# Down products of three FFN phases by seven block products instead of eight, with the upper halves' low parts by accumulating DMA

## The chip, the cores and the metric

The kernel runs as one program on one core of a Trainium2 chip. The metric is its device time in microseconds. The kernel before took 1877.66 us, the median of three runs (1875.56 to 1878.22).

## The reference, cut to what matters

Two layers over 528 tokens (16 learned meta tokens and 512 of the sequence) of width 1024; each layer has two SwiGLU half steps (FFNs) with a mixer between them, and a layer norm after each of the three. The change touches only the FFNs, four in all. D_FF is 2816, that is 22 hidden tiles of 128.

```python
def swiglu(x, w_gate, w_up, w_down):
    return (jax.nn.silu(x @ w_gate) * (x @ w_up)) @ w_down

for l in range(DEPTH):
    h = layer_norm(a * h + 0.5 * swiglu(h, ffn1_w_gate[l], ffn1_w_up[l], ffn1_w_down[l]), ln1_g[l], ln1_b[l])
    ...   # projection, causal pooling, gated linear attention, w_out
    h = layer_norm(a * h + y, ln2_g[l], ln2_b[l])
    h = layer_norm(a * h + 0.5 * swiglu(h, ffn2_w_gate[l], ffn2_w_up[l], ffn2_w_down[l]), ln3_g[l], ln3_b[l])
return h[:, N_META:]
```

## The kernel before

Everything is stored transposed: 8 blocks of 128 channels on the partitions, tokens along the free axis. Each float32 operand is split into a high part (the value copied to fp32r) and a low part (value minus high part), and each product is three matmuls: high x high, high x low, low x high. The last FFN computes only the 512 own tokens (span OWN), the other three all 528 (span ALL, in two halves of 264).

Weights come as one stream of pieces of 128 x 1024 floats (512 KB). SP loads them into two raw buffers (`raw`, L337), each as soon as the piece that was in it is split; ScalarE makes the high part in one of four slots of `w_hi` (`high_part`, L927) once the piece four before is used up; the low part comes from VectorE (L1280, pieces of the fast pairs), from GpSimd by a subtraction (L358, the classic gate and up pieces and all down pieces), or, for mixer pieces and the first four of an FFN, by ScalarE writing the negated weights into `w_lo` (L933) and GpSimd issuing a DMA that adds the weights from memory (L351).

An FFN goes through its 22 hidden tiles in three phases (8, 8, 6). For each tile m of a phase it computes gate and up, silu(gate) x up is the hidden tile (`prod`, then `h_hi`, `h_lo`), and at the end of the phase the down products of its tiles are added into X, eight output rows mo with all three matmuls for each tile (L411 to L413). Tiles 0 to 3 are classic: 96 matmuls a pair of gate and up. From tile 4 on a pair is a fast pair (`fast_pair`): the 2 x 2 block product of (gate, up) weights, each cut into a lower and an upper half of four channel blocks, with (early, late) halves of the tokens is made with seven products of 12 matmuls instead of eight. That wants four sums of weight blocks per pair (`w_sums`, VectorE; high parts by ScalarE L921, low parts by VectorE L1285), four sums of token blocks once per FFN (`v_sum`), and sums of the products in PSUM: ScalarE copies p1, u2 and p5 (L968, L980, L983), VectorE adds to c22 (L1337) and c12 (L1344). TensorE waits for p1_copied before its third product, u2_copied before the fifth, p5_copied before the sixth and c22_done before the seventh.

Each engine's order is written out by hand in its `ffn`: during pair i ScalarE and VectorE prepare the weights of pair i + 1 and finish the hidden tile of pair i - 1. `F22` and the counts in the waits number the tiles, `piece_done` the pieces that TensorE has used up. After the last phase the down rows end in `resid`, which also adds up the statistics for the layer norm.

Of the kernel before, what the change touches and what calls it, by code (L numbers as in the profile page):

```python
# [6 lines left out]

# [21 lines left out]
PHASES = ((0, 8), (8, 8), (16, 6))  # L29
# [27 lines left out]
FFN_PIECES = 2 * MT + len(PHASES) * KC  # L57
# [16 lines left out]
CLASSIC = 4  # L74
BAND = 4
BLOCK = BAND * P
FAST = MT - CLASSIC
# [24 lines left out]
def fast_index(l, f, m):  # L102

    return (2 * l + f) * FAST + m - CLASSIC


def whole(n):

    r = n % LAYER_PIECES
    if FFN_PIECES <= r < FFN_PIECES + MIX_IN + MIX_OUT:  # L110
        return True
    r -= 0 if r < FFN_PIECES else FFN_PIECES + MIX_IN + MIX_OUT
    for p, (m0, nm) in enumerate(PHASES):
        at = 2 * m0 + KC * p
        if at <= r < at + 2 * nm:
            return m0 + (r - at) // 2 < CLASSIC
    return True


def by_dma(n):  # L120

    r = n % LAYER_PIECES
    return n >= SLOTS and (r < SLOTS or FFN_PIECES <= r < FFN_PIECES + MIX_IN + MIX_OUT + SLOTS)


def lo_value(n):

    same = [i for i in range(n % SLOTS, n + 1, SLOTS) if by_dma(i) == by_dma(n)]
    return len(same) * (16 if by_dma(n) else 1)


def negated(n):

    return sum(by_dma(i) for i in range(n + 1))
# [38 lines left out]
def build(nc, x_t, stream, params, out_t):  # L173
    ctx = ExitStack()
    with ctx:
# [12 lines left out]
        x_lo = sb("x_lo", [P, KC, T], F32R)  # L188
# [33 lines left out]
        with ExitStack() as s4:  # L222
            v_sum = sb("v_sum", [P, 4, BAND, HALF], F32, s4)
        with ExitStack() as s5:
            s_hi = sb("s_hi", [P, 4, BLOCK], F32R, s5)
            s_lo = sb("s_lo", [P, 4, BLOCK], F32R, s5)
# [7 lines left out]
        with ExitStack() as s3:  # L234
            h_hi = sb("h_hi", [P, TILES, T], F32R, s3)
            h_lo = sb("h_lo", [P, TILES, T], F32R, s3)
            silu = sb("silu", [P, T], F32, s3)
# [3 lines left out]
            p5_copy = sb("p5_copy", [P, 2, HALF], F32, s3)  # L241
            u2_copy = sb("u2_copy", [P, 2, HALF], F32, s3)
# [37 lines left out]

        def matmul_parts(ps, span):
# [18 lines left out]
            s_sum_done s_hi_done s_lo_done v_sum_done v_hi_done v_lo_done""".split()  # L300
# [9 lines left out]

        def wait_piece(eng, n):

            eng.wait_ge((lo_added if by_dma(n) else lo_done)[n % SLOTS], lo_value(n))
# [10 lines left out]
        def _(sp):  # L324
# [7 lines left out]
            for n in range(SLOTS + RAWS, DEPTH * LAYER_PIECES):  # L332
                if by_dma(n - RAWS):
                    sp.wait_ge(S["raw_neg"], negated(n - RAWS))
                else:
                    wait_piece(sp, n - RAWS)
                sp.dma_start(raw[:, n % RAWS, :], stream[n // RAWS, n % RAWS]).then_inc(raw_full[n % RAWS], 16)  # L337
# [8 lines left out]
        def _(pool):  # L346
            def add_raw(n):

                slot = n % SLOTS
                pool.wait_ge(S["raw_neg"], negated(n))  # L350
                pool.dma_start(w_lo[:, slot, :], stream[n // RAWS, n % RAWS],  # L351
# [39 lines left out]
            for n in range(SLOTS, DEPTH * LAYER_PIECES):  # L391
                if n % LAYER_PIECES == FFN_PIECES + SLOTS:
                    pad(n // LAYER_PIECES)
                if by_dma(n):
                    add_raw(n)
                elif whole(n):
# [9 lines left out]
        def _(pe):  # L406
# [61 lines left out]
            def fast_product(o, hi, lo, rhs_hi, rhs_lo, start, stop):  # L468

                for k in range(BAND):  # L470
                    w = slice(k * P, (k + 1) * P)
                    nc.tensor.matmul(o, hi[:, w], rhs_hi[:, k, :], start=start and k == 0, stop=False,  # L472
                                     skip_group_check=True)
                    nc.tensor.matmul(o, hi[:, w], rhs_lo[:, k, :], start=False, stop=False, skip_group_check=True)  # L474
                    m = nc.tensor.matmul(o, lo[:, w], rhs_hi[:, k, :], start=False, stop=stop and k == BAND - 1,  # L475
                                         skip_group_check=True)
                return m

            def fast_pair(l, f, m, gate, span):
# [7 lines left out]
                low, high = slice(0, BLOCK), slice(BLOCK, 2 * BLOCK)  # L487
                g, u = gate % SLOTS, (gate + 1) % SLOTS
                x_low = (x_hi[:, 0:BAND, early], x_lo[:, 0:BAND, early])
                x_high = (x_hi[:, BAND:KC, early], x_lo[:, BAND:KC, early])  # L490
                x_late = (x_hi[:, BAND:KC, late], x_lo[:, BAND:KC, late])

                def mixed(j):
                    return v_hi[:, j - 1, :, 0:n], v_lo[:, j - 1, :, 0:n]

                def summed(j):
                    pe.wait_ge(S["s_lo_done"], 4 * i + j)
                    return s_hi[:, j - 1, :], s_lo[:, j - 1, :]

                wait_piece(pe, gate)  # L500
                fast_product(u0, w_hi[:, g, low], w_lo[:, g, low], *x_low, True, True).then_inc(S["p1_acc"], 1)
                pe.wait_ge(S["v_lo_done"], 4 * (2 * l + f) + 4)
                fast_product(g1, *summed(1), *mixed(1), True, True).then_inc(S["p5_acc"], 1)
                pe.wait_ge(S["p1_copied"], i + 1)
# [1361 lines left out]
```

## Time and profile before

| | |
|---|---|
| median of 3 runs | 1877.66 us (1875.56 to 1878.22) |
| profiled execution | 1878.16 us, its span 1876.4 us |
| mean granted TensorE clock | 0.991 of full speed |
| TensorE, matmuls | 1838.4 us busy, 14406 |
| VectorE | 1179.2 us busy, 1837 instructions |
| ScalarE | 881.3 us busy, 1357 |
| GpSimd | 351.7 us busy, 206 |
| DMA | 206.73 MB, 110 GB/s over the span |
| raw loads | 316 of 512 KB, 3.8 us from issue to landing (median) |
| accumulating loads | 60 of 512 KB, 7.8 us |

The page is one execution as the hardware profiler recorded it. Matmuls overlap in their pipeline, so the distance between two starts says what one costs, not its recorded duration; the same holds to a lesser degree for VectorE and ScalarE, whose instructions start before the one ahead has ended. In the rows, PE is TensorE, DVE VectorE, ACT ScalarE, POOL GpSimd, SPq the DMA queue of SP; `x2` in a timeline row are two instructions of that line back to back.

### The profile page before, as it was taken

The numbers are of one execution on the slowest core, as the hardware profiler recorded it, in microseconds if no ns is written. First come the engines' busy times: TensorE is split into PE (matmuls) and PEld (weight loads), VectorE is DVE, ScalarE is ACT, GpSimd is POOL, SyncE is SP. The second block draws the span as 40 slices with busy tenths as digits, with TensorE's granted clock in tenths as the row PEclk, the third lists the DMA queues.
The fourth block names the chain that finished last, engine by engine and source line by source line (L and its number), as shares of the span: only waits on it lengthen the run. The fifth ranks groups of instructions, "written<-read, shape, count | busy, mean of one in ns | idle before, by whom it ended". The sixth has DMA issues, their size and how long they took to land.

```text
span 1876.4 us, 34684 instructions
## 1 busy us (share of the span) xinstructions
PE 1838.4 (98%) x14406; PEld 1768.9 (94%) x14406; DVE 1179.2 (63%) x1837; ACT 881.3 (47%) x1357; POOL 351.7 (19%) x206
## 2 busy tenths in 40 slices
PE   8999999999999999999999999999999999999997
PEld 7999999999999999999999999999998879899895
DVE  5828638568547827728477286375684587285575
ACT  4524525474346524525465245254743465254353
POOL 3040220411002040130420302104110120303113
PEclk9999999999999999999999999999999999999998
DMA  4223323556554332332542333226565633333232
GB/s 158 102 90 113 102 81 111 154 121 132 112 126 97 103 103 91 106 93 96 144 103 102 91 113 107 89 99 158 128 134 113 133 89 102 99 109 119 82 111 90
DMA packets 57469, 206.73 MB, mean 110 GB/s; under 512 B 6368, under 2 KB 6368, under 8 KB 57312
## 3 DMA queue, kind: packets, MB, share of 16 engines
q1 hardware_dynamic: 48240, 171.78, 29.6%
q0 software_dynamic: 8640, 31.46, 9.2%
q8 instruction: 115, 1.88, 0.4%
q10 hardware_dynamic: 432, 1.25, 0.2%
q14 instruction: 42, 0.34, 0.1%
HBM read 202.38 MB, written 2.10 MB: 109 GB/s over the span
## 4 chain that ended last, share of the span: by engine, by line
PE 90%; DVE 5%; ACT 2%; DMA 1%; issue 1%; ACTq 0%; DVEq 0%
PE PS L472 12%; PE PS L475 12%; PE PS L474 12%; PE PS L411 9%; PE PS L412 9%; PE PS L413 9%; PE PS L452 5%; PE PS L453 5%; PE PS L454 5%; PE PS L443 2%; PE PS L421 2%; PE PS L422 2%; PE PS L737 1%; DMA raw<-in_stream 1%; ACT X L1064 1%
## 5 line engine op out<-in xcount | busy, mean ns | idle before, releaser
L358 POOL TENSOR_TENSOR w_lo<-raw,w_hi 128x1024 fp32r<-128x1024 f32 x112 | 282.1, 2523 | 1086.1 <-ACT w_hi L927 1059.8
L411 PE MATMUL PS<-h_hi,w_hi 128*128 128x264 f32 (+1 forms) x1238 | 370.2, 299 | 0.6 <-DVE h_lo L1219 0.3
L412 PE MATMUL PS<-h_lo,w_hi 128*128 128x264 f32 (+1 forms) x1238 | 369.7, 299 | 0.0
L413 PE MATMUL PS<-h_hi,w_lo 128*128 128x264 f32 (+1 forms) x1238 | 369.4, 298 | 0.0
L927 ACT ACTIVATE w_hi<-raw 128x1024 fp32r<-128x1024 f32 x240 | 215.1, 929 | 232.4 <-PE PS L413 179.2
L472 PE MATMUL PS<-v_hi,s_hi 128*128 128x264 f32 (+1 forms) x864 | 244.9, 283 | 0.2 <-ACT PS L968 0.2
L474 PE MATMUL PS<-v_lo,s_hi 128*128 128x264 f32 (+1 forms) x864 | 244.3, 283 | 0.0
L475 PE MATMUL PS<-v_hi,s_lo 128*128 128x264 f32 (+1 forms) x864 | 243.9, 282 | 0.0
L411 PEld LDWEIGHTS PS<-h_hi,w_hi 128*128 128x128 f32 x1238 | 233.0, 188 | 9.2 <-DVE h_lo L1219 1.7
L412 PEld LDWEIGHTS PS<-h_lo,w_hi 128*128 128x128 f32 x1238 | 233.1, 188 | 7.3
L413 PEld LDWEIGHTS PS<-h_hi,w_lo 128*128 128x128 f32 x1238 | 232.3, 188 | 7.3
L921 ACT ACTIVATE s_hi<-s_sum 128x512 fp32r<-128x512 f32 x288 | 177.9, 631 | 100.2 <-PE PS L475 96.1
L452 PE MATMUL PS<-x_hi,w_hi 128*128 128x264 f32 (+1 forms) x696 | 208.1, 299 | 1.7 <-ACT s_r L1154 1.6
L453 PE MATMUL PS<-x_lo,w_hi 128*128 128x264 f32 (+1 forms) x696 | 205.9, 296 | 0.0
L454 PE MATMUL PS<-x_hi,w_lo 128*128 128x264 f32 (+1 forms) x696 | 205.6, 295 | 0.0
L1285 DVE TENSOR_TENSOR s_lo<-s_sum,s_hi 128x512 fp32r<-128x512 f32 x288 | 190.3, 686 | 16.5 <-ACT s_hi L921 15.9
L475 PE MATMUL PS<-x_hi,w_lo 128*128 128x264 f32 (+1 forms) x576 | 163.1, 283 | 0.0
L472 PEld LDWEIGHTS PS<-v_hi,s_hi 128*128 128x128 f32 x864 | 162.5, 188 | 0.4 <-ACT PS L968 0.4
L474 PEld LDWEIGHTS PS<-v_lo,s_hi 128*128 128x128 f32 x864 | 162.9, 189 | 0.0
L472 PE MATMUL PS<-x_hi,w_hi 128*128 128x264 f32 (+1 forms) x576 | 162.7, 283 | 0.0
L475 PEld LDWEIGHTS PS<-v_hi,s_lo 128*128 128x128 f32 x864 | 162.4, 188 | 0.0
L474 PE MATMUL PS<-x_lo,w_hi 128*128 128x264 f32 (+1 forms) x576 | 161.5, 280 | 0.0
(231 smaller groups left out, 4107.8 us busy)
## 6 DMA issues: line engine op xcount, KB each, us to landing
raw<-in_stream SPq DMA_DIRECT2D x316, 512.0 KB, 3.8
w_lo<-in_stream POOLq DMA_DIRECT2D x60, 512.0 KB, 7.8
raw_first<-in_stream SPq DMA_DIRECT2D x4, 512.0 KB, 5.9
out_t<-X SPq DMA_DIRECT2D x8, 256.0 KB, 2.1
X<-in_x_t SPq DMA_DIRECT2D x7, 264.0 KB, 7.5
par<-in_params ACTq DMA_DIRECT2D x2, 480.0 KB, 3.5
X<-in_x_t ACTq DMA_DIRECT2D x1, 264.0 KB, 4.8
```

Source lines behind the costliest of these rows:

```text
L358: nc.gpsimd.tensor_tensor(w_lo[:, slot, :], raw[:, slot % RAWS, :], w_hi[:, slot, :].bitcast(F32), ALU.subtract).then_inc(lo_done[slot], 1)
L411: nc.tensor.matmul(o, hi, rhs_hi[:, k, tok], start=first, stop=False)
L412: nc.tensor.matmul(o, hi, rhs_lo[:, k, tok], start=False, stop=False)
L413: return nc.tensor.matmul(o, lo, rhs_hi[:, k, tok], start=False, stop=last)
L452: yield nc.tensor.matmul(o, hi, rhs_hi[:, k, tok], start=k == 0, stop=False)
L453: yield nc.tensor.matmul(o, hi, rhs_lo[:, k, tok], start=False, stop=False)
L454: yield nc.tensor.matmul(o, lo, rhs_hi[:, k, tok], start=False, stop=k == n - 1)
L472: nc.tensor.matmul(o, hi[:, w], rhs_hi[:, k, :], start=start and k == 0, stop=False, skip_group_check=True)
L474: nc.tensor.matmul(o, hi[:, w], rhs_lo[:, k, :], start=False, stop=False, skip_group_check=True)
L475: m = nc.tensor.matmul(o, lo[:, w], rhs_hi[:, k, :], start=False, stop=stop and k == BAND - 1, skip_group_check=True)
L927: nc.scalar.activation(w_hi[:, n % SLOTS, part], raw[:, n % RAWS, part], ACT.Copy).then_inc(S["raw_hi"], 1)
L1285: V.tensor_tensor(s_lo[:, j - 1, :], s_sum[:, j - 1, :], s_hi[:, j - 1, :].bitcast(F32), ALU.subtract).then_inc(S["s_lo_done"], 1)
```

## The change

The phases become (6, 6, 6, 4). The down products of the first three phases are also made as 2 x 2 block products: two output rows (mo = 2q and 2q + 1) against the early and late tokens, with the phase's six tiles cut into those with an even and those with an odd place (three each). A phase has four such down pairs of 7 x 9 = 63 matmuls. They take the place of a pair in `FAST_ORDER`, one pair later than the phase's last tile: the first gate and up pair of the next phase comes before them. So each engine runs one loop over 30 fast pairs of an FFN, 18 of gate and up and 12 down. Down pairs need the weight sums as the others do (three blocks of 128 wide), and four sums of each pair of hidden tiles (`t_sums`), with their high and low parts (`t_hi`, `t_lo`). Their results go into X by two VectorE instructions (`add_down`). The last phase's four tiles stay classic, two rows to a piece.

The low parts of the upper halves of a fast pair's weights come in the other way: ScalarE writes the negated half (`negative`), GpSimd issues an accumulating DMA of that half (256 KB, 192 KB for a down pair); VectorE makes only the gate's lower half. SP's reload waits for the negated half and for the weight sums too. `p5_copy` and `u2_copy` have one buffer instead of two; raw hidden tiles share storage with their low parts.

```diff
-PHASES = ((0, 8), (8, 8), (16, 6))
+PHASES = ((0, 6), (6, 6), (12, 6), (18, 4))
+def fast_order():
+    order = []
+    for p, (m0, nm) in enumerate(PHASES):
+        order += [("up", m, 0) for m in range(CLASSIC if p == 0 else m0 + 1, m0 + nm)]
+        if p < FAST_DOWNS:
+            order.append(("up", m0 + nm, 0))
+            order += [("down", p, q) for q in range(PAIRS)]
+    return order
 @@ SP
+                if dma_adds(was):
+                    sp.wait_ge(S["raw_neg"], negated(was))
+                if engine_splits(was):
+                    wait_low(sp, was)
+                if kind_of(was) in ("gate", "up"):
+                    sp.wait_ge(S["s_sum_done"], 4 * fast_index(*place_of(was)) + (4 if kind_of(was) == "gate" else 2))
+                part = slice(0, width(n))
 @@ GpSimd
-                pool.dma_start(w_lo[:, slot, :], stream[n // RAWS, n % RAWS],
+                pool.dma_start(w_lo[:, slot, part], stream[n // RAWS, n % RAWS, :, part],
                                accum_op=ALU.add).then_inc(lo_added[slot], 16)
 @@ TensorE, fast_pair
+                wait_low(pe, gate)
+                if kind == "down":
+                    pe.wait_ge(S["h_lo_done"], l * 44 + 22 * f + sum(PHASES[a]))
                 ...                                     # p1
+                    pe.wait_ge(S["t_lo_done"], thirds_index(l, f, sum(PHASES[a]) - 1) + 1)
                 ...                                     # p5, p6
+                wait_added(pe, gate)
                 ...                                     # g0 with the gate's upper half, p7, p3
-                wait_piece(pe, gate + 1)
+                wait_added(pe, gate + 1)
                 pe.wait_ge(S["c22_done"], i_all + 1)
 @@ ScalarE, in fast pair i
                     act.wait_ge(S["p1_acc"], i_all + 1)
                     ...                                 # copy p1
+                    if was == "up":
+                        act.wait_ge(S["c12_done"], i_all)
+                        silu_of(2 - ps, layout)
+                    if follows:
+                        gate_high(fast_piece(l, f, i + 1))          # high part, then negated upper half
                     ...                                 # copies u2, p5
+                    if follows:
+                        up_high(fast_piece(l, f, i + 1) + 1)        # upper half: high part, negated
+                        for j in range(1, 4):
+                            sum_high(l, f, i + 1, j)
+                    if was == "up" and kind == "up":
+                        hidden_high(l, f, was_a, span)
+                    elif was == "down" and kind == "up":
+                        act.wait_ge(S["piece_done"], fast_piece(l, f, i))
+                        hidden_high(l, f, sum(PHASES[was_a]), span)
+                    if follows:
+                        sum_high(l, f, i + 1, 4)
 @@ VectorE
+            def t_sums(l, f, m, span):                  # after the product of each tile with odd place
+                V.tensor_tensor(t[2], b22, b12, ALU.subtract).then_inc(S["t_sum_done"], 1)
+                V.tensor_tensor(t[0], b11, b12, ALU.subtract).then_inc(S["t_sum_done"], 1)
+                dve.wait_ge(S["t_sum_done"], 4 * at + 1)
+                V.scalar_tensor_tensor(out=t[1], in0=t[2], scalar=-1.0, in1=b11, op0=ALU.mult, op1=ALU.subtract)
+                dve.wait_ge(S["t_sum_done"], 4 * at + 3)
+                V.scalar_tensor_tensor(out=t[3], in0=t[1], scalar=-1.0, in1=b21, op0=ALU.mult, op1=ALU.subtract)
+            def add_down(l, f, i, span):
+                for odd, op in enumerate((ALU.add, ALU.subtract)):
+                    x, y = halves(X[:, 2 * q + odd, :], halved(span)), pair(ps + odd, halved(span))
+                    ...                                 # ALPHA * x op y in phase 0, x op y after it
 @@ VectorE, in fast pair i
+                    if was == "down":
+                        add_down(l, f, i - 1, span)
+                    if follows:
+                        w_sums(l, f, i + 1)
+                    if was == "up":
+                        fast_prod(l, f, was_a, 2 - ps, span)        # and t_sums at an odd place
+                    if follows:
+                        gate_low(fast_piece(l, f, i + 1))           # lower half only
+                        sum_low(l, f, i + 1, 1)
                     ...                                 # c22, sum_low 2 and 3, c12
+                    if was == "up" and kind == "up":
+                        hidden_low(l, f, was_a, span)
+                    elif was == "down" and kind == "up":
+                        hidden_low(l, f, sum(PHASES[was_a]), span)
+                    if follows:
+                        sum_low(l, f, i + 1, 4)
 @@ TensorE, end of an FFN
+                last_down(0, range(nm - 1))
+                last_down(1, range(nm - 1))             # two rows before the last tile is wanted
+                last_down(0, [nm - 1]).then_inc(S["last_acc"], 1)
+                last_down(1, [nm - 1]).then_inc(S["piece_done"], 1)
```

## Rows read from the trace of the kernel before

**Rows 1.** First part of the page: busy us (share of the span) x instructions.

```profile
PE 1838.4 (98%) x14406; PEld 1768.9 (94%) x14406; DVE 1179.2 (63%) x1837; ACT 881.3 (47%) x1357; POOL 351.7 (19%) x206
```

**Rows 2.** Fourth part of the page: the chain that ended last, by engine.

```profile
PE 90%; DVE 5%; ACT 2%; DMA 1%; issue 1%; ACTq 0%; DVEq 0%
```

**Rows 3.** Waits of TensorE, whole span: waiting <- releaser: total us, times, longest.

```profile
PE PS L421 <- DVE w_lo L1781: 8.9, 3, 7.9
...
PE PS L472 <- DVE PS L1337: 1.1, 1, 1.1
```

**Rows 4.** Window, first FFN: length, busy us of each engine, clock, DMA.

```profile
30.00:340.00 310.00, 309.92 (x2559) 309.70 (x2558) 195.53 (x283) 140.46 (x237) 59.97 (x24) 1.00 0.31 100
```

**Rows 5.** Timeline, ScalarE's copy of p1: start us, us, instruction, idle before.

```profile
70.86 0.38 ACT L968 ACTIVATE PS<-PS 128x264 f32<-128x264 f32 x1 [2.22 <-PE PS L475]
...
81.05 0.38 ACT L968 ACTIVATE PS<-PS 128x264 f32<-128x264 f32 x1 [2.22 <-PE PS L475]
...
1654.00 0.37 ACT L968 ACTIVATE PS<-PS 128x256 f32<-128x256 f32 x1 [2.11 <-PE PS L475]
...
1663.81 0.37 ACT L968 ACTIVATE PS<-PS 128x256 f32<-128x256 f32 x1 [2.11 <-PE PS L475]
```

**Rows 6.** Timeline of VectorE, down rows added into X, two FFNs.

```profile
105.77 0.70 DVE L1365 SCALAR_TENSOR_TENSOR X<-X,PS 128x528 f32<-128x528 f32 x1 [2.17 <-PE PS L413]
111.57 0.70 DVE L1365 SCALAR_TENSOR_TENSOR X<-X,PS 128x528 f32<-128x528 f32 x1 [5.10 <-PE PS L413]
...
1609.38 0.69 DVE L1365 SCALAR_TENSOR_TENSOR X<-X,PS 128x512 f32<-128x512 f32 x1 [4.87 <-PE PS L413]
1614.94 0.69 DVE L1365 SCALAR_TENSOR_TENSOR X<-X,PS 128x512 f32<-128x512 f32 x1 [4.87 <-PE PS L413]
```

**Rows 7.** Timeline of VectorE, one pair of gate and up, first FFN.

```profile
70.67 0.69 DVE L1266 TENSOR_TENSOR s_sum<-raw 128x512 f32<-128x512 f32 x1 [1.30 <-DMA raw<-in_stream]
...
73.28 0.70 DVE L1214 SCALAR_TENSOR_TENSOR prod<-PS,silu 128x528 f32<-128x528 f32 x1
73.89 1.82 DVE L1280 TENSOR_TENSOR w_lo<-raw,w_hi 128x1024 fp32r<-128x1024 f32 x2
75.63 0.69 DVE L1285 TENSOR_TENSOR s_lo<-s_sum,s_hi 128x512 fp32r<-128x512 f32 x1
76.23 0.70 DVE L1219 TENSOR_TENSOR h_lo<-prod,h_hi 128x528 fp32r<-128x528 f32 x1
76.85 0.43 DVE L1337 TENSOR_TENSOR PS<-PS,p_copy 128x264 f32<-128x264 f32 x1
77.19 1.28 DVE L1285 TENSOR_TENSOR s_lo<-s_sum,s_hi 128x512 fp32r<-128x512 f32 x2
...
80.10 0.69 DVE L1266 TENSOR_TENSOR s_sum<-raw 128x512 f32<-128x512 f32 x1 [0.55 <-DMA raw<-in_stream]
```

**Rows 8.** Timeline of ScalarE, same pair.

```profile
71.64 1.58 ACT L927 ACTIVATE w_hi<-raw 128x1024 fp32r<-128x1024 f32 x2
...
74.33 0.63 ACT L921 ACTIVATE s_hi<-s_sum 128x512 fp32r<-128x512 f32 x1
74.85 0.65 ACT L909 ACTIVATE h_hi<-prod 128x528 fp32r<-128x528 f32 x1
```

**Rows 9.** Landing: raw loads 60:340, raw loads 395:505, accumulating loads.

```profile
DMA to landing us min/median/max: 3.3/3.7/6.1
...
DMA to landing us min/median/max: 3.8/4.2/9.6
...
DMA to landing us min/median/max: 6.5/7.8/10.4
```

**Rows 10.** Timeline of VectorE, first fast pair of the first FFN.

```profile
66.49 0.44 DVE L1337 TENSOR_TENSOR PS<-PS,p_copy 128x264 f32<-128x264 f32 x1
```

**Rows 11.** Timeline of VectorE, end of the first phase.

```profile
101.44 2.16 DVE L1219 TENSOR_TENSOR h_lo<-prod,h_hi 128x528 fp32r<-128x528 f32 x1 [0.71 <-ACT h_hi L909]
```

**Rows 12.** Timeline of GpSimd, same stretch.

```profile
100.62 2.40 POOL L358 TENSOR_TENSOR w_lo<-raw,w_hi 128x1024 fp32r<-128x1024 f32 x1 [2.24 <-ACT w_hi L927]
```

More of the change, by code:

```diff
@@ L8 @@
+import itertools
 from contextlib import ExitStack
@@ L126, in lo_value, with high_half, low_half, dma_adds @@
+def high_half(n):
+    return slice(width(n) // 2, width(n))
+def low_half(n):
+    return slice(0, width(n) // 2)
+def dma_adds(n):
+    return kind_of(n) != "split"
+def engine_splits(n):
+    return kind_of(n) in ("split", "gate")
+def added_value(n):
+    return 16 * sum(dma_adds(i) for i in range(n % SLOTS, n + 1, SLOTS))
 def lo_value(n):
-    same = [i for i in range(n % SLOTS, n + 1, SLOTS) if by_dma(i) == by_dma(n)]
-    return len(same) * (16 if by_dma(n) else 1)
+    return sum(engine_splits(i) for i in range(n % SLOTS, n + 1, SLOTS))
@@ L132, in negated @@
+NEGATED = list(itertools.accumulate(dma_adds(i) for i in range(DEPTH * LAYER_PIECES)))
 def negated(n):
-    return sum(by_dma(i) for i in range(n + 1))
+    return NEGATED[n]
 def stream_ready(l, idx):
@@ L332, in _ @@
             for n in range(SLOTS + RAWS, DEPTH * LAYER_PIECES):
[L333 to L337, printed above, removed]
+                was = n - RAWS
+                if dma_adds(was):
[5 more added lines that the diff above has]
+                part = slice(0, width(n))
+                sp.dma_start(raw[:, n % RAWS, part], stream[n // RAWS, n % RAWS, :, part]).then_inc(raw_full[n % RAWS], 16)
             for k in range(KC):
@@ L496, in summed @@
                 def summed(j):
[L497 to L502, printed above, removed]
+                    pe.wait_ge(S["s_lo_done"], 4 * i_all + j)
+                    w = slice(0, nb * P)
+                    return s_hi[:, j - 1, w], s_lo[:, j - 1, w]
@@ new lines, in ffn @@
+                for k in range(KC):
+                    chunk_products(LN, k, 3, FP, span)
+                wait_piece(pe, FP + 3)
+                product(3, 3, x_hi, x_lo, KC, span=span).then_inc(S["piece_done"], 1)
+                for m in range(2, CLASSIC):
+                    gate = FP + 2 * m
+                    for j in range(2):
+                        wait_piece(pe, gate + j)
+                        pe.wait_ge(S["prod_done" if j else "silu_done"], F22 + m - 1)
+                        product(2 * (m % 2) + j, (gate + j) % SLOTS, x_hi, x_lo, KC, span=span)\
+                            .then_inc(S["piece_done"], 1)
@@ L1007, in ffn @@
+                act.wait_ge(S["c12_done"], fast_index(l, f, FAST))
+                silu_of(2 * ((FAST - 1) % 2), layout)
+                whole_high(last + 2)
+                hidden_high(l, f, MT - 1, span)
+                whole_high(last + 3)
                 if f == 0:
@@ new lines, in product_of @@
+            def product_of(l, f, m, ps, layout, span, scale):
+                if m > 0 and not is_high(m):
+                    dve.wait_ge(S["t_sum_done"], 4 * min(thirds_index(l, f, m), (2 * l + f + 1) * FAST_DOWNS * THIRDS))
+                V.scalar_tensor_tensor(out=halves(hidden(m, span), layout), in0=pair(ps + 1, layout), scalar=scale,
+                                       in1=halves(silu, layout), op0=ALU.mult, op1=ALU.mult).then_inc(S["prod_done"], 1)
+                if is_high(m) and phase_of(m) < FAST_DOWNS:
+                    t_sums(l, f, m, span)
```

635 lines of the change are left out of this document (333 added, 302 removed).

## The prediction

> **What bounds the kernel now.** I read the busy shares first: TensorE is busy for 98% of the span, twice ScalarE's share and one and a half times VectorE's [rows 1]. Then the chain that ended last: 90% of it is TensorE [rows 2]. Then who TensorE waited for: the longest entry, 8.9 us, is the start of the program, and a wait on VectorE's sum inside the pairs occurs once, 1.1 us [rows 3]. The window over the first FFN says the same, 309.92 of 310 us busy at clock 1.00 [rows 4]. So an FFN costs its matmuls times their pitch, and two pitches follow from the starts of one instruction that recurs in each pair:
> - a pair of 84 matmuls of 264 columns: 81.05 - 70.86 = 10.19 us, 0.1213 each; of 256 columns (last FFN): 1663.81 - 1654.00 = 9.81 us, 0.1168 each [rows 5];
> - a classic down row: 111.57 - 105.77 = 5.80 us for 8 x 6 = 48 matmuls of 264, 0.1208 each; in the last FFN 1614.94 - 1609.38 = 5.56 us for 24 of 512 columns, 0.2317 each [rows 6].
>
> **TensorE's share of the change.** Down before: 22 hidden tiles x 8 rows x 6 = 1056 matmuls, 127.6 us. After: 12 down pairs of 7 x 3 x 3 = 63 matmuls, 756 x 0.1213 = 91.7 us, and the last four tiles as before, 192 x 0.1208 = 23.2; together 114.9. Saved 12.7 us in each of three FFNs, 38.1. Last FFN: 528 x 0.2317 = 122.3 before, 756 x 0.1168 + 96 x 0.2317 = 88.3 + 22.2 = 110.5 after: 11.8 (256 columns are a little dearer per column than 512). Sum 49.9 us. Gate and up keep their matmuls. The profiled execution took 1878.16 us (span 1876.4), 0.5 above the median of the runs, so with TensorE never waiting it would take 1828.3.
>
> **Whether the others can feed it.** Now every pair, a down pair of 63 x 0.1213 = 7.64 us too, wants weight sums, splits and copies in its own time; before, the down rows left VectorE and ScalarE mostly idle. Prices are distances between starts.
> - VectorE, up pair [rows 7]: sums of the next weights 2.61 (70.67 to 73.28), product 0.61, low parts of 1536 columns 1.74, low part of a sum 0.60 (75.63 to 76.23) x 4, low part of h 0.62, two PSUM sums 0.34 (76.85 to 77.19) x 2: 8.66 of 10.19. The upper halves' low parts by DMA take 1.14 off, leaving 0.60. A tile with even place splits only its early half (0.35). One with odd place adds four hidden sums of 264, 4 x 0.35 plus two waits on the instruction just ahead at 0.18 each (the 2.61 above is 4 x 0.60 and one such wait), 1.76, and the low part of 1056 columns, 1.2 on the line through 264 columns (0.34) and 512 (0.60). So 7.3 and 10.4 us alternate, mean 8.9 under 10.19.
> - VectorE, down pair: 384 columns lie between 264 (0.34) and 512 (0.60), 0.47. Adding two rows into X 1.24, sums 4 x 0.47 + 0.18, low part of gate 0.47, of sums 1.88, PSUM sums 0.68: 6.3 of 7.64.
> - ScalarE [rows 8], estimated from 0.52 for 512 columns (74.33 to 74.85) and 1.5 for 1536: up pair: three PSUM copies 0.85, silu 0.5, high parts 1.5, now two negated halves 1.04, sums 2.08, h 0.54, and every other time 1.0 for hidden sums: 6.5 or 7.5 of 10.19. Down pair: 4.5, 5.0 with a silu, of 7.64.
> - GpSimd: its splits of the down weights go; two DMA issues a pair come. Nothing waits for its arithmetic in the pairs.
>
> Averages fit, so the order within a pair decides. Times from here on are counted from the pair's first matmul; a product of seven takes 1.46 us in an up pair and 1.09 in a down pair. The tightest place is VectorE's PSUM sum c22, which TensorE wants before its seventh product, 8.73 us into an up pair. With an odd tile VectorE has before it 2.61 + 0.61 + 1.76 + 0.60 + 0.60 and 0.44 for itself, 6.6 us: it holds if the raw weights are there by 2.1 us into the pair. In a down pair (limit 6.55) it has 2.06 + 0.61 + 0.47 + 0.47 + 0.44 = 4.05, so they may come at 2.5. ScalarE's copy u2, behind the high and the negated part of the gate weights, holds with raw gate weights at 3.9 us (down 2.8). The low parts for the first down pair come late: the last tile's high parts end about 9.4 us into the pair before, its t_lo at 10.9, wanted at 10.19 + 1.09 = 11.3. I take 0 for it, ends 0 and 1 us at 12 places.
>
> **The raw buffers.** Two buffers make a loop: weights land, VectorE sums and splits, SP reloads. Before: 4.96 us of VectorE and 4.4 of loading (75.7, end of the split, to 80.10 [rows 7]), 9.4 of 10.19. SP's queue now also waits for the sums and the negated half; the latter, behind p5's copy, ends at 6.0 us in an up pair and 4.7 in a down pair. VectorE's part becomes 3.8 or 5.6, mean 4.7, so the loop closes if loading takes under 5.5 us. How long loading takes with two accumulating DMAs a pair beside it no row shows. Bounds: the first FFN, without them, 3.3/3.7/6.1 us; a stretch of the mixer, where each raw load starts with an accumulating one of 512 KB, 3.8/4.2/9.6 [rows 9]. The step is 0.5, so I take 4.4 + 0.5 = 4.9 for the second of two, ends 3.3 and 6.1 (9.6 was one in a stretch). Raw weights then come 0.7 to 2.0 us into a pair: nothing waits, with a margin of one microsecond or less.
>
> The accumulating DMA itself took 6.5/7.8/10.4 us for 512 KB [rows 9]. For 256 KB of an up pair it starts 3.8 us into the pair before and is wanted at 10.19 + 4.36 = 14.5, so 10.7 us are there for it. For 192 KB of a down pair it starts at 2.6 to 3.1 and is wanted at 7.64 + 3.27 = 10.9: 7.8 us just holds, and I take about 6.5, the least of the row, since the bytes are fewer; cost 0, the other end is rival D.
>
> The DMA loads are the place where a rule speaks against the change. "DMA: Bandwidth & Descriptors" in the Trainium skill (Rules for kernel authors) says that streams issued from SP, ACT and GpSimd run on the same 16 engines and interleave, so that bytes added on one queue delay the other. The 3.7 and 4.2 us above agree; by the rule alone, without a size, it is the mechanism of rival C.
>
> **FFN start.** The one place where VectorE has no slack today: the first fast pair starts at 69.41 - 10.19 = 59.2 us (70.86 less 12 matmuls), its seventh product at 67.95, and c22 runs from 66.49 to 66.93 without having waited [rows 10]. The change puts two sets of hidden sums (tiles 1 and 3) and their low parts before it, 2 x (1.76 + 1.2) = 5.9, and takes off 2 x 1.14 and 2 x 0.27, 2.8: 3.1 us net, done at 70.0, 2.1 late; waits that VectorE has there anyway hide some of it. I take 1.5 us in each of four FFNs, 6.0; ends 0 and 4 each, because GpSimd's split of a classic piece runs there: a low part of h took 2.16 us [rows 11] beside such a split [rows 12] against 0.62. That is what "SBUF — State Buffer" in the Trainium skill (Who interferes with whom) states: a VectorE instruction with two SBUF inputs and a GpSimd one that reads SBUF exclude each other. By it the sum here would be about 2.4 us (one split) more per FFN, 1845; by the row above, 1836.
>
> Last phase: rows of 24 matmuls take 2.9 us; VectorE needs 0.62 x 3 a row, 1.9, so it does not set the pace; the change interleaves two rows ahead of the last tile, which gives 4.4 us for that tile's product and split; cost 0. Stray slow loads: 1.5 us for all, as the one wait of 1.1 of before and a little more.
>
> Sum: 1828.3 + 6.0 + 1.5 = 1835.8; forecast **1836**, -2.2%.
>
> **Rivals.**
> - A, as forecast: 0.60.
> - B, VectorE's order stalls: c22 after hidden sums, and the first down pair, 28 + 12 = 40 places at 0.6 us: 1860. For it: margins of 1 and 0.4 us. Against: every estimate of its inputs would have to be a microsecond late. 0.20.
> - C, slower: raw loading becomes the bound. From 5.5 us on each pair lengthens by the excess; at about 5.9 us the gain is used up. At 6.1 (the largest of the first FFN) 72 up pairs lose 0.6 = 43, and 48 down pairs (384 KB, say 5.5 us, with 2.5 of VectorE against 7.64) 0.4 = 19: 1898. For it: bytes moved rise from 206.73 MB to about 259 (36 x 256 KB and 24 x 192 KB accumulated per FFN). Against: medians of 3.7 and 4.2. 0.10.
> - D, the accumulating DMAs of down pairs are late, 8.7 us instead of under 7.8: 0.9 x 48 = 43, so 1879, no change. 0.06.
> - E, the change does more than I think: the FFN starts hide their work and no load strays, 1828. 0.04.
>
> **Numbers.** Faster holds A, B, E and a little of D, 0.85; within 0.2% (what a measurement of this kernel can tell from none, 3.8 us) 0.04; slower 0.11. The range 1825 to 1864 leaves out C, D and the tail of B.
>
> **What would show it.** Pitch of down pairs 7.64 us by the p1 copy, VectorE's adds into X in couples 7.6 apart; TensorE's waits still small, most of them L472-like for c22 at the first fast pair of each FFN, 1 to 2 us each; raw loads near 4.9 us. Wrong: waits for w_lo from the stream (D), VectorE's sums waiting for raw with TensorE waiting behind (C), c22 waits in every other up pair (B), or a pitch of down matmuls other than 0.121.

## The result, and the profile after

The changed kernel takes 1966.74 us (median of 4 runs, 1962.33 to 1972.82) against 1877.21 for the kernel before beside it (1875.56 to 1878.22): ratio 1.048, 95% interval 1.046 to 1.049. Forecast was 1836, -2.2%; it came out at +4.8%. The profiled execution took 1962.33 us, its span 1960.6. Of e7 below, one of four runs took 2501.5 us at a granted clock of 0.652 and is left out of its row.

First part of the page (busy us, share of the span, instructions), two of its DMA queues (packets, MB, share of 16 engines), and the chain by engine:

```profile
PE 1839.4 (94%) x14400; PEld 1767.2 (90%) x14400; DVE 1412.5 (72%) x2505; ACT 1128.8 (58%) x1985; POOL 356.6 (18%) x366
...
q0 software_dynamic: 43200, 88.10, 28.2%
q1 hardware_dynamic: 50544, 167.59, 27.0%
...
PE 38%; DMA 30%; DVE 17%; issue 9%; ACT 3%; SPq 2%; POOL 1%; DVEq 0%; ACTq 0%
```

TensorE still has the most busy time, but of the chain that ended last it holds 38% where it held 90% [rows 2]; 30% is now DMA, and 17% VectorE. TensorE is busy 1839.4 us for 14400 matmuls, about as long as before [rows 1], though the work was to shrink by 49.9 us. 121.2 us of the span are idle, 83.2 more than the 38.0 of before. Who TensorE waits for, in the form of [rows 3]:

```profile
PE PS L561 <- DVE PS L1528: 59.2, 60, 3.2
PE PS L561 <- ACT u_copy L1120: 17.0, 23, 1.5
```

The first is the wait for c22, VectorE's sum of two products: 60 times where it was once. VectorE itself waits, ahead of its sums of the next weights, for the raw load (first row before, second row after), and so does ScalarE for its high parts (after):

```profile
DVE s_sum L1266 <- DMA raw<-in_stream: 41.7, 46, 2.8
```

```profile
DVE s_sum L1461 <- DMA raw<-in_stream: 257.0, 113, 4.7
```

```profile
ACT w_hi L1065 <- DMA raw<-in_stream: 97.8, 77, 2.7
```

The window of the first FFN [rows 4] has 19.4 us less of TensorE, in a stretch where the DMA engines moved 135 GB/s (100 before):

```profile
30.00:340.00 310.00, 290.54 (x2315) 285.61 (x2314) 237.78 (x423) 188.33 (x367) 60.70 (x62) 0.99 0.57 135
```

From issue to landing, first FFN, raw loads and then accumulating ones (min, median, max; 3.3/3.7/6.1 before for raw [rows 9]):

```profile
DMA to landing us min/median/max: 3.2/5.2/7.4
```

```profile
DMA to landing us min/median/max: 3.3/3.8/6.5
```

VectorE over two pairs, where one pair of before was [rows 7]:

```profile
128.89 1.31 DVE L1418 SCALAR_TENSOR_TENSOR X<-X,PS 128x528 f32<-128x528 f32 x2
132.61 0.69 DVE L1461 TENSOR_TENSOR s_sum<-raw 128x512 f32<-128x512 f32 x1 [2.41 <-DMA raw<-in_stream]
...
135.22 0.69 DVE L1477 TENSOR_TENSOR w_lo<-raw,w_hi 128x512 fp32r<-128x512 f32 x1
...
136.42 0.43 DVE L1528 TENSOR_TENSOR PS<-PS,p_copy 128x264 f32<-128x264 f32 x1
...
138.65 0.68 DVE L1483 TENSOR_TENSOR s_lo<-s_sum,s_hi 128x512 fp32r<-128x512 f32 x1
143.22 0.69 DVE L1461 TENSOR_TENSOR s_sum<-raw 128x512 f32<-128x512 f32 x1 [3.89 <-DMA raw<-in_stream]
```

At 135.22 it splits the lower half of the gate weights, which gives the buffer back at about 135.8; the next sums start at 143.22, 3.89 us of that idle. So buffer to buffer the load took 7.4 us. For the eight such places in a row that end with this one (from 68 us on) the distance is 6.3, 5.6, 5.4, 6.3, 6.7, 7.1, 6.8 and 7.4 us, mean 6.4, where the prediction had 4.9 and its loop closed at 5.5. c22 stands behind the sums in VectorE's order, so it shifts with them, and TensorE waits ahead of its seventh product.

### The profile page after: what moved, and what is told of

It reads as the page before. It is cut to its first block, busy times and chain, and to the rows that moved or that the text cites. A ratio compares the mean times of both kernels' runs of the same rounds, so it can differ in the third digit from the quotient of the medians.

```text
span 1960.6 us, 37276 instructions
## 1 busy us (share of the span) xinstructions
PE 1839.4 (94%) x14400; PEld 1767.2 (90%) x14400; DVE 1412.5 (72%) x2505; ACT 1128.8 (58%) x1985; POOL 356.6 (18%) x366
## 3 DMA queue, kind: packets, MB, share of 16 engines
q0 software_dynamic: 43200, 88.10, 28.2%
## 4 chain that ended last, share of the span: by engine, by line
PE 38%; DMA 30%; DVE 17%; issue 9%; ACT 3%; SPq 2%; POOL 1%; DVEq 0%; ACTq 0%
DMA raw<-in_stream 30%; PE PS L540 4%; PE PS L541 4%; PE PS L542 4%; DVE s_sum L1467 3%; PE PS L561 3%; DVE w_lo L1477 3%; PE PS L562 3%; PE PS L563 3%; PE PS L499 2%; PE PS L501 2%; PE PS L500 2%; PE PS L509 2%; PE PS L510 2%; PE PS L531 2%
## 5 line engine op out<-in xcount | busy, mean ns | idle before, releaser
L439 POOL DMA_DIRECT2D w_lo<-in_stream x300 | 255.8, 853 | 1411.1 <-ACT w_lo L1058 1367.7
L1483 DVE TENSOR_TENSOR s_lo<-s_sum,s_hi 128x512 fp32r<-128x512 f32 (+1 forms) x480 | 292.2, 631 | 17.2 <-ACT s_hi L1054 16.8
L1054 ACT ACTIVATE s_hi<-s_sum 128x512 fp32r<-128x512 f32 (+1 forms) x480 | 261.4, 585 | 50.9 <-PE PS L563 48.1
L1065 ACT ACTIVATE w_hi<-raw 128x1024 fp32r<-128x1024 f32 (+3 forms) x272 | 221.7, 815 | 98.8 <-DMA raw<-in_stream 97.8
L1461 DVE TENSOR_TENSOR s_sum<-raw 128x512 f32<-128x512 f32 (+1 forms) x120 | 76.7, 639 | 257.1 <-DMA raw<-in_stream 257.0
L1108 ACT ACTIVATE PS<-PS 128x264 f32<-128x264 f32 (+1 forms) x120 | 44.8, 373 | 294.8 <-PE PS L563 294.8
L1058 ACT ACTIVATE w_lo<-raw 128x512 fp32r<-128x512 f32 (+2 forms) x300 | 202.7, 676 | 0.0
L540 PEld LDWEIGHTS PS<-x_hi,w_hi 128*128 128x128 f32 x696 | 131.1, 188 | 7.4 <-issue 4.2
L541 PEld LDWEIGHTS PS<-x_lo,w_hi 128*128 128x128 f32 x696 | 131.2, 188 | 2.7
L542 PEld LDWEIGHTS PS<-x_hi,w_lo 128*128 128x128 f32 x696 | 130.6, 188 | 2.8
```

Of the source, the lines that this page charges most:

```text
L439: pool.dma_start(w_lo[:, slot, part], stream[n // RAWS, n % RAWS, :, part], accum_op=ALU.add).then_inc(lo_added[slot], 16)
L540: yield nc.tensor.matmul(o, hi, rhs_hi[:, k, tok], start=k == 0, stop=False)
L541: yield nc.tensor.matmul(o, hi, rhs_lo[:, k, tok], start=False, stop=False)
L542: yield nc.tensor.matmul(o, lo, rhs_hi[:, k, tok], start=False, stop=k == n - 1)
L1054: nc.scalar.activation(s_hi[:, j - 1, w], s_sum[:, j - 1, w], ACT.Copy).then_inc(S["s_hi_done"], 1)
L1058: nc.scalar.activation(w_lo[:, n % SLOTS, part], raw[:, n % RAWS, part], ACT.Copy, scale=-1.0)\
```

## The experiments

The theory, T1: two raw buffers are a loop (land, sum, split, reload); beside the accumulating DMAs a load is so long that a turn of the loop takes longer than a pair, and VectorE passes this on to TensorE by c22. The rival, T2: VectorE's own added work and its order make c22 late. Runs of one group (e1 to e4, e5 to e8, f and g, h) share the runs of the kernel before, 1877.2, 1876.2, 1876.8 and 1876.1 us. The raw landing is that of loads issued between 60 and 340 us; the waits are those of the whole span.

| kernel | us | ratio to before (95%) | raw landing 60:340, median | VectorE's raw waits, us |
|---|---|---|---|---|
| changed | 1966.7 | 1.046 to 1.049 | 5.2 | 257.0 |
| e1 16 columns added | 1845.2 | 0.982 to 0.985 | 3.7 | 33.0 |
| e2 gate split first | 1924.3 | 1.023 to 1.028 | 5.2 | 199.9 |
| e3 hidden sums late | 1942.6 | 1.034 to 1.037 | 5.4 | 229.7 |
| e4 low parts by VectorE | 1870.7 | 0.996 to 0.998 | 3.7 | 39.7 |
| e5 same bytes, not added | 1869.6 | 0.995 to 0.999 | 4.3 | 135.1 |
| e6 e4, splits first | 1864.0 | 0.991 to 0.995 | 3.6 | 28.5 |
| e7 up halves alone by DMA | 1905.6 | 1.014 to 1.018 | 4.6 | 123.1 |
| e8 up halves by GpSimd | 1916.9 | 1.020 to 1.023 | 3.7 | 61.0 |
| f1 three raw buffers | 1849.5 | 0.983 to 0.986 | 5.5 | 66.1 |
| f2 e6, three buffers | 1851.7 | 0.985 to 0.988 | 3.6 | none listed |
| f4 f2, hidden sums late | 1874.3 | 0.998 to 1.000 | 3.7 | 0.2 |
| g1 adding alone, in before | 1905.9 | 1.012 to 1.017 | 5.2 | 161.8 |
| h1 f1, gate split first | 1847.4 | 0.983 to 0.986 | 5.2 | 44.3 |
| h2 f1, 16 columns added | 1844.9 | 0.981 to 0.984 | 3.6 | 1.7 |
| h3 up's adding held | 1933.1 | 1.025 to 1.034 | 4.8 | 187.0 |
| h4 h3, gate split first | 1928.2 | 1.025 to 1.030 | 5.6 | 178.5 |

**e1, the bytes taken away.**

```diff
-  part = slice(0, PIECE) if kind_of(n) == "added" else high_half(n)
+  part = slice(0, PIECE) if kind_of(n) == "added" else slice(width(n) // 2, width(n) // 2 + 16)
```

> The changed kernel, but each accumulating DMA of a fast pair adds 16 columns instead of the whole upper half (512 or 384); the rest of that low part stays the negated copy, so its value is left out. Instructions, waits and the number of DMAs are the same; some 55 MB of accumulating bytes go. T1 (the two raw buffers' loop is late because a load takes 5 to 7 us beside the accumulating bytes): loading falls back to about 4.4 us, TensorE's wait on the c22 sum (59.2 us) to under 10, the time to 1836-1855. T2 (VectorE's own work and order are late, the loads only look late): 1950-1967. If the half-clock stretches follow the stalls, they fall from 84 us to about 37 with T1.

1845.2. The same instructions and waits, the same work of VectorE (1418.0 us busy against 1412.5), and 121 us less: T2 as the main cause is out, the loss hangs on the added bytes. The expectation on the clock missed: the mean is 0.984 here, 59 us at half clock and not 37, although TensorE idles 40.1 us, as little as before (38.0). Of the raw loads in the first FFN, and TensorE's wait for c22:

```profile
DMA to landing us min/median/max: 2.9/3.7/4.9
```

```profile
PE PS L561 <- DVE PS L1528: 3.0, 12, 0.4
```

The Trainium skill's "DMA: Bandwidth & Descriptors" (Rules for kernel authors) has it that DMAs issued from SP, ACT and GpSimd all run on the same 16 engines and interleave. That one queue's bytes delay the other's follows from this, and the traces agree: 5.2 against 3.7 us.

**e2 and e3, the buffer given back earlier.** e2 moves `gate_low(next)` ahead of `fast_prod(...)`; e3 calls `t_sums` right behind c22 instead of inside the product.

> The changed kernel with one order changed on VectorE: the low part of the gate weights ahead of the product and its hidden sums, so that the raw buffer is given back 0.6 us (even tile) or 2.4 us (odd tile) earlier after an up pair; the work ahead of c22 is the same. T1: up pairs keep pace again (2.9 us of VectorE + 6 us of loading under 10.19), down pairs still don't (2.5 + 5.5 over 7.64); 1880-1915. T2: nothing ahead of c22 changed, 1950-1970.

> The changed kernel with the four hidden sums of an odd tile (1.8 us) moved behind c22. T1: the raw gate buffer is given back 1.8 us earlier in every other up pair, half of what the other order gives: 1910-1935. T2: c22 stands 1.8 us earlier in those pairs: 1870-1900.

1924.3 and 1942.6. e2 moves nothing past c22 and gains 42 us, as only T1 says; e3 takes 1.8 us from ahead of c22 in every other up pair and gains 24, about half of e2. That this is T1's proportion is in part luck, since e3 also pays a wait that the changed kernel has with 2.2 us only, for the low part of a hidden tile:

```profile
PE PS L561 <- DVE h_lo L1389: 13.1, 12, 1.1
```

Both end 8 to 9 us above the upper bound that I gave T1. The down pairs, which neither touches, may cost more than I had allowed; no run separates them.

**e4, the part with sevens alone.**

```diff
 def dma_adds(n):
-    return kind_of(n) != "split"
+    return kind_of(n) == "added"
 def engine_splits(n):
-    return kind_of(n) in ("split", "gate")
+    return kind_of(n) != "added"
 ...   # no negated copies; ScalarE's up_high() ahead of its copies
 # gate_low(): the whole gate piece, and the upper half of up, by VectorE
```

> The down products by sevens kept, the other part undone: upper halves' low parts of the pairs by VectorE, no accumulating DMA in the pairs, no negated copies; 1.1 us more of VectorE a pair, ahead of the gate buffer's release. T1: loads back at 4.4 us against 4.1 to 6.7 us of VectorE in the loop: 8.5 and 10.3 of 10.19, down pairs 3.4 + 4.2 of 7.64, so nearly in pace: 1845-1885. T2: VectorE has more before c22 in every pair: 1980-2020.

1870.7, as T1 had it: VectorE is busy 1537.0 us, 124 more than in the changed kernel, with more ahead of c22, and the time is 96 us less.

**e5, the same bytes without the addition.**

```diff
+  adds = {"accum_op": ALU.add} if kind_of(n) == "added" else {}
   pool.dma_start(w_lo[:, slot, part], ...,
-                 accum_op=ALU.add)
+                 **adds)
```

> The changed kernel, but the DMAs of the fast pairs' upper halves overwrite the low part instead of adding to it: the same bytes, descriptors and waits, no accumulation (the low part then holds the weight itself, so that value is left out). T1a (the bytes alone delay the raw loads): 1955-1970 as the changed kernel. T1b (it is the adding: 88.1 MB on the accumulating queue took 28.2% of the 16 engines and 167.6 MB of plain loads 27.0%, so a byte added costs twice): the delay halves or better, loads at about 4.2 us, 1855-1900.

1869.6, T1b: of the 121 us between the changed kernel and e1, 97 hang on the adding and 24 on the bytes. The time that the queue's packets took shows it too: 88.10 MB again, but 21.1% of a span of 1868.0, 394 us of all 16 engines, against 28.2% of 1960.6, 553 us:

```profile
q0 software_dynamic: 8640, 31.46, 9.2%
```

```profile
q0 software_dynamic: 43200, 88.10, 21.1%
```

The first row is the kernel before, the second e5. Only 56.6 of the 88.1 MB are no longer added. Less the 173 us that the kernel before's 31.46 MB take (9.2% of its 1876.4), 56.6 MB cost 380 us added and 221 plain: 6.7 against 3.9 us of all engines per MB. In f1, by the same sum, it is 6.3 added.

**e6, e7, e8: who makes the upper halves' low parts.** In all three the splits stand ahead of the product. e6: VectorE both; e7: up's by accumulating DMA, gate's by VectorE; e8: up's by GpSimd (`split(n)` on `high_half(n)`), gate's by VectorE.

> Down products by sevens, the upper halves' low parts by VectorE (no accumulating DMA in the pairs), and all low parts of the weights ahead of the product and its hidden sums. T1: the loop is 2.6 + 1.7 + 4.2 = 8.5 us in every up pair against 10.3 in every other one before this order; VectorE's raw waits (39.7 us) halve and the time falls from 1870.7 to 1850-1862. T2 (VectorE is now simply full, 82%): 1866-1875.

> Down products by sevens, only the up weights' upper half by accumulating DMA (28 MB instead of 57), the gate weights' whole low part by VectorE ahead of the product. T1 with a delay in proportion to the accumulating bytes: loads at about 4.4 us median, 1845-1870. If the delay comes from any one accumulating DMA meeting a load, whatever the sum of bytes: loads at 5 us in every pair, 1890-1920.

> Down products by sevens, no accumulating DMA in the pairs, the up weights' upper half by a GpSimd subtraction (about 1.3 us from 2.4 to 2.6 for 1024 columns), the gate weights' low part by VectorE ahead of the product. If the two engines work beside each other: 0.6 us less of VectorE a pair than with all low parts on it, 1843-1858. If they exclude each other: up to 1.3 us a pair more for VectorE than by itself, and the time 1870-1910.

1864.0, 1905.6, 1916.9. e6 gains 7 on e4 by order; it lies between my two ranges, and the raw waits fell from 39.7 to 28.5 us, not to half. Half the added bytes of e2 (e7) cost 42 us over e6, all of them (e2) 60. My 1845 to 1870 for e7 was wrong, and the other range, 1890 to 1920, held (with loads at 4.6 us, not 5). But e7 differs from e2 in a second way, the gate's upper half is split by VectorE inside the loop (0.6 us), so its 42 us are not the price of the bytes alone. e8 has e6's raw landings (3.7 and 3.6 us) and no added bytes in the pairs; it ends 7 us above the range I gave for engines that exclude each other. VectorE's sums are longer in it. Sums of 512 columns in the first FFN, e8 and then e6 (instruction, count, busy us, mean ns, idle before):

```profile
L1468 DVE TENSOR_TENSOR s_sum<-s_sum,raw 128x512 f32<-128x512 f32 x17 | 19.9, 1171 | 1.8
L1465 DVE TENSOR_TENSOR s_sum<-s_sum,raw 128x512 f32<-128x512 f32 x17 | 18.2, 1071 | 0.0
```

```profile
L1467 DVE TENSOR_TENSOR s_sum<-s_sum,raw 128x512 f32<-128x512 f32 x17 | 11.8, 692 | 1.8
...
L1464 DVE TENSOR_TENSOR s_sum<-s_sum,raw 128x512 f32<-128x512 f32 x17 | 11.6, 684 | 0.0
```

A sum of two SBUF inputs takes 1.07 or 1.17 us instead of 0.69 where GpSimd subtracts beside it. The rule of the Trainium skill's "SBUF — State Buffer" (Who interferes with whom) that the prediction used agrees. The raw waits rise as well, from 28.5 to 61.0 us; the up buffer is now given back by GpSimd, whose subtraction of an upper half took 1.4 us there (median). How the 53 us between e8 and e6 divide over the two no run tells.

**f1, f2, f4: three buffers.** Room: even hidden tiles keep only their early half in a packed array, and `kdec` and `state` share a place.

```diff
-RAWS = 2
+RAWS = 3
-  raw[:, n % RAWS, ...]
+  raw[:, (n - SLOTS) % RAWS, ...]
```

> The changed kernel with three raw buffers instead of two (room from packing the hidden tiles closer and letting two mixer arrays share a place); accumulating DMAs and all orders as changed. T1 (the loop over two buffers closes late): a load now starts a buffer ahead, so loads of 5 to 7 us are covered; 1840-1875. T2' (the 16 DMA engines are simply too full beside accumulating): 1930-1960.

> Down products by sevens, all low parts of the pairs' weights by VectorE and ahead of the product (no accumulating DMA in the pairs), and three raw buffers. With two buffers this order took 1864.0 with 28.5 us of raw waits on VectorE; if those waits are what is left of the loop: 1840-1852. If VectorE's own work (83% busy) sets it: 1855-1864.

> As three raw buffers with all low parts by VectorE, and the four hidden sums of an odd tile moved behind c22. VectorE's order as the rest: 1836-1848, at least 4 us under the same kernel with the hidden sums ahead. If its sum of work sets it or the first down pairs' t_lo comes late: no gain or a loss of up to 10.

1849.5, 1851.7, 1874.3. f1 adds every byte that the changed kernel adds, its loads land even later, and it is 117 us faster: it beats the kernel before by 1.5%. The packing that makes the room is not what gains: with 16 columns added, two buffers and no packing took 1845.2 us (e1), three and packing 1844.9 (h2). Page, window of the first FFN, waits and landing:

```profile
PE 1799.8 (98%) x14400; PEld 1746.0 (95%) x14400; DVE 1418.2 (77%) x2505; ACT 1127.8 (61%) x1985; POOL 359.5 (20%) x366
...
PE 86%; DVE 6%; ACT 3%; issue 2%; DMA 2%; ACTq 0%; DVEq 0%; SPq 0%
```

```profile
30.00:340.00 310.00, 308.05 (x2533) 307.29 (x2533) 256.21 (x449) 204.60 (x396) 70.39 (x68) 1.00 0.63 149
```

```profile
PE PS L570 <- DVE PS L1540: 3.9, 14, 0.6
```

```profile
DVE s_sum L1473 <- DMA raw<-in_stream: 66.1, 59, 3.8
```

```profile
DMA to landing us min/median/max: 3.4/5.5/8.4
```

VectorE still waits 66.1 us for raw weights, but TensorE sees 3.9 of it. That is the theory in one comparison: not a long load, a load longer than the loop allows. f4 missed both of its ranges, a gain or a loss of up to 10 us: it lost 22.6 us to f2. TensorE then waits, as in e3, for low parts of the first down pair's hidden tiles,

```profile
PE PS L570 <- DVE h_lo L1397: 13.1, 12, 1.1
```

and for c22 31 times instead of 15 (9.9 and 4.4 us). So moving the hidden sums behind c22 gives TensorE nothing where loads are not late, and it wasn't by c22's place in the order that e3 gained.

**g1, the adding alone.** The kernel before with `add_raw` for upper halves, the negated copies on ScalarE behind p5's copy, and the waits on SP's queue as in the change.

> The kernel before with only the second part of the change: upper halves' low parts of the fast pairs by accumulating DMA (36 pairs in each of two FFNs a layer become 18 here, classic down rows as before). T1: loop 2.6 + 0.6 + 0.6 us of VectorE and 5 to 6 us of loading, 9.3 of 10.19 in every up pair, no short down pairs: near even, 1878-1900. So the loss of the whole needs both parts. If adding beside the loads is enough by itself: above 1910. If it only takes work off VectorE: 1870-1877.

(What I wrote in brackets is a slip: g1 has the 72 pairs of before.) 1905.9, above my bound of 1900 for T1, and below the 1910 of the alternative: the adding costs 29 us without any short down pair, so "needs both parts" was wrong. ScalarE's p1 copy:

```profile
70.58 0.38 ACT L1011 ACTIVATE PS<-PS 128x264 f32<-128x264 f32 x1 [3.03 <-PE PS L515]
...
82.02 0.38 ACT L1011 ACTIVATE PS<-PS 128x264 f32<-128x264 f32 x1 [3.27 <-PE PS L515]
...
93.20 0.38 ACT L1011 ACTIVATE PS<-PS 128x264 f32<-128x264 f32 x1 [3.23 <-PE PS L515]
```

Pairs of this phase are 11.4 and 11.2 us long, not 10.19 [rows 5]; those of the next phase are 10.2 to 10.7. So one part loses 29 us, the other gains 12 (e6) or 6 (e4), and both together lose 90. The likely reason is that the down pairs want their loads (384 KB each) within 7.6 us; no run isolates them.

**h1 to h4.** h3 and h4 make GpSimd wait, ahead of the up weights' accumulating DMA, for the next pair's raw gate weights: `wait_raw(pool, n + 2)`. h1 is f1 with e2's order, h2 is f1 with e1's columns.

> The changed kernel, two buffers, all bytes added as in it, but GpSimd holds the accumulating DMA of a pair's up weights until the next pair's raw gate weights have landed; it then runs from about 2 to 6 us into the pair, wanted at 8.7 (down pair 6.5), instead of beside the two raw loads. If a load is long because an adding DMA runs at the same moment: raw loads back to about 4.3 us median, 1890-1935. If it is the sum of bytes: 1955-1970. If the held DMA is late for TensorE: above 1970, with waits on w_lo from the stream.

> The same hold with the gate weights' low part ahead of the product (1924.3 without the hold). Overlap as the cause: 1870-1900. Sum of bytes: 1915-1930.

> Three raw buffers, all adding as changed, and the gate weights' low part ahead of the product; without that order 1849.5 with 66 us of raw waits on VectorE of which TensorE saw 3.9. If any of it still reaches TensorE, 1842-1847; if the loop is fully covered, 1848-1851.

> Three raw buffers and only 16 columns of each upper half added (the rest of those low parts stays the negated copy). The floor of this design: neither the loop nor the adding is left. With two buffers and 16 columns it took 1845.2; so 1838-1845. Anything above 1828.3 is VectorE's order, ScalarE's copies and the clock, not loads.

1933.1, 1928.2, 1847.4, 1844.9. Holding gains 34 us over the changed kernel, inside the range for an overlap, though loads landed in 4.8 us and not 4.3. It gains nothing over e2 (h4: 3.9 more, intervals overlapping), where loads landed in 5.6 us, no sooner, and that is the range for the sum of bytes. The held DMAs are also late for TensorE, a cost of their own that I had looked for only above 1970 us (h3, then h4):

```profile
PE PS L563 <- DMA w_lo<-in_stream: 10.2, 16, 1.3
```

```profile
PE PS L563 <- DMA w_lo<-in_stream: 14.3, 23, 1.6
```

So whether it is the meeting in time or the engines' whole load that lengthens a raw load stays open. h1 and f1 can't be told apart. h2, which leaves most of the upper halves' low parts out, is 4.6 us under f1 and 2.4 under h1, with overlapping intervals: with three buffers the adding costs at most some 5 us.

## Why the prediction was wrong

**The step that failed** is the loading time in "The raw buffers": "so I take 4.4 + 0.5 = 4.9". It measured 5.4 to 7.4, mean 6.4. Two things are in it: the median of one load went from 3.7 to 5.2, where I had taken the mixer's 4.2 [rows 9] as the like case, and the second of two, which the sums need, came 1.2 us after that and not 0.7. Why the pairs are worse than that stretch of the mixer, with half the added bytes for each load, no run tells. The margin to 5.5 was 0.6 us, smaller than the ignorance I had written down (3.3 to 6.1), and I gave what lies beyond it 0.10. The step also left something out: a limit for the down pairs. By its own terms 7.64 less 2.5 of VectorE leaves 5.1 us for a load, and the four loads of 384 KB among the eight places took 5.6, 5.4, 6.3 and 6.7. The step also had a right half: which loop, its VectorE part (3.8 or 5.6 us; 77.89 + 0.6 - 74.66 = 3.8 at one place), and which wait would show it, those of rival C.

**Rival C's price** was too small too: 1898 at 6.1 us. With 6.4 in its own formula it gives 72 x 0.9 + 48 x 0.7 = 98, an estimate of 1934, still 32 short. Between the changed kernel and f1, with the same work, lie 117.2 us of span: 77.6 idle (121.2 against 43.6), and 39.6 in which TensorE is busy with the same 14400 matmuls (1839.4 against 1799.8). No term of the sum had the latter. Part of it may be the clock. Here it is around the longest stall of the first FFN, 2.41 us ahead of the matmul at 149.86 (length, busy us of PE, PEld, DVE, ACT and POOL, clock, DMA, GB/s):

```profile
149.86 0.36 PE L561 MATMUL PS<-v_hi,w_hi 128*128 128x264 f32 x1 [2.41 <-DVE PS L1528]
```

```profile
149.00:152.00 3.00, 2.14 (x14) 2.17 (x15) 3.00 (x7) 0.80 (x2) 0.00 (x0) 0.84 0.73 233
152.00:156.00 4.00, 4.00 (x26) 4.00 (x25) 3.90 (x6) 1.48 (x3) 0.00 (x0) 0.69 0.23 91
156.00:160.00 4.00, 4.00 (x36) 4.00 (x35) 1.76 (x4) 3.38 (x8) 1.34 (x2) 1.00 0.38 45
```

After the stall TensorE works at a granted 0.69 for four microseconds, a mixture of 2.4 and 1.2 GHz, and is back at 1.00 from 156 us on. Over the span the clock is 0.979, which is 2 x 0.021 x 1960.6 = 82 us at the lower level, against 34 before (0.991) and 48 in f1 (0.987): 34 us at half speed more than f1, 17 us lost. The other 22 of the 39.6 I can't assign. And the 17 hold for this execution alone: the other three runs of the changed kernel had clocks of 0.982 to 0.985 and took 4 to 10 us longer. In e3 TensorE idled 107.2 us at a mean clock of 0.987, f1's, and was still busy 24.2 us longer than in f1. So the kernels with more stalls have more matmul time, and the mean clock accounts for less than half of it; the rest stays open.

**TensorE's share**: f1 shows the pitch. ScalarE's p1 copy, two down pairs of the first and of the last FFN:

```profile
98.26 0.38 ACT L1119 ACTIVATE PS<-PS 128x264 f32<-128x264 f32 x1 [1.62 <-PE PS L572]
...
105.93 0.38 ACT L1119 ACTIVATE PS<-PS 128x264 f32<-128x264 f32 x1 [1.61 <-PE PS L572]
```

```profile
1661.04 0.37 ACT L1119 ACTIVATE PS<-PS 128x256 f32<-128x256 f32 x1 [1.65 <-PE PS L572]
...
1668.55 0.37 ACT L1119 ACTIVATE PS<-PS 128x256 f32<-128x256 f32 x1 [1.62 <-PE PS L572]
...
1715.19 0.37 ACT L1119 ACTIVATE PS<-PS 128x256 f32<-128x256 f32 x1 [2.31 <-PE PS L572]
...
1725.16 0.37 ACT L1119 ACTIVATE PS<-PS 128x256 f32<-128x256 f32 x1 [1.60 <-PE PS L572]
```

A down pair takes 7.67 us (7.64 forecast) and 7.51 in the last FFN (63 x 0.1168 = 7.36). Against the kernel before TensorE's busy time fell by 38.6, not 49.9: 14 us more at half clock are 7 of the difference, and up pairs of 9.97 instead of 9.81 us in the last FFN another 3 over 18 pairs.

**FFN start**, 6.0 us: the size is near, the mechanism was another. All of f1's c22 waits are 3.9 us, the longest 0.6. But TensorE waits once in each FFN for ScalarE's copy of p1 (0.2 us, once, in the kernel before), which in ScalarE's order stands behind the high part of the hidden sums:

```profile
PE PS L570 <- ACT PS L1119: 4.2, 4, 1.4
```

```profile
60.11 1.08 ACT L1045 ACTIVATE t_hi<-t_raw 128x1056 fp32r<-128x1056 f32 x1 [0.97 <-DVE t_raw L1389]
61.10 0.37 ACT L1119 ACTIVATE PS<-PS 128x264 f32<-128x264 f32 x1
```

The prediction went through the order at the start of an FFN for VectorE alone, and priced ScalarE by its sum of work in a pair. **VectorE and ScalarE**: averages fit as computed (VectorE 77% in f1). **Rival B** is out (e1, f4), with about 4 us of it in f1. **Rival D** is out: accumulating DMAs landed in 3.8 us in the first FFN (longest 6.5), and no wait of TensorE in the changed kernel names w_lo from the stream; I had taken 6.5. **Stray loads** at 1.5 us was the failed step again. With a third buffer the change gives what its matmuls promise but for 19 to 21 us: 1847.4 (h1) and 1849.5 (f1) against 1828.3. In f1's profiled execution (1845.1 us, 16.8 above) 11.3 us are TensorE time that was not saved and 5.6 are idle time beyond the 38.0 of before. So with loads as forecast the 1836 would still have been 11 to 14 us low.

## What to carry to other kernels

When a change shortens the period of a loop that refills a few buffers and adds traffic beside the refill, price the loop by the slowest loads and not by their median, and for the shortest pair too. If the margin is smaller than the spread of the rows, the slower side deserves more than the 0.10 it had here. A load that is longer than the loop allows cost more than its excess here: beside 77.6 us of idle time TensorE was busy 39.6 us longer with the same matmuls. Try one more buffer before judging such a change; here it turned +4.8% into -1.5%, with a median load no faster than before. And look at every engine's order at the start of a loop, not at the busiest engine's alone.

## What the runs showed of the hardware

- Adding in a DMA costs the engines about 1.6 to 1.7 times a plain transfer from the same queue (6.3 in f1 and 6.7 in the changed kernel against 3.9 in e5, us of all 16 per MB), and it, more than its bytes, slows the loads beside it: 5.2, 4.3 and 3.7 us median with adding, with plain bytes and without either.
- With half the added bytes (e7) the raw loads landed in 4.6 us, with all of them (e2) in 5.2, with none (e6) in 3.6 (medians, first FFN).
- An accumulating DMA of 256 or 192 KB landed in 3.8 us (3.3 to 6.5) in the first FFN of the changed kernel, under the 6.5 to 10.4 of 512 KB [rows 9]; in f1, which moves the same bytes in less time, it took 4.6 (3.4 to 8.7).
- Giving GpSimd the subtraction of the upper halves beside VectorE's sums cost 53 us against VectorE doing it all (e8 against e6); a sum of 512 columns went from 0.69 to 1.07 or 1.17 us.
